# Splitting a turned table row group by two ScalarE copies and a GpSimd subtraction, in a two-block transformer kernel on one Trainium2 core

## The reference

```
def peer(xn, wq, subkeys, u, v):
    q = (xb @ wq).reshape(t, PEER_HEADS, 2, PEER_DQ // 2)
    s = jnp.einsum('thpd,hpkd->thpk', q, subkeys)
    ...                                   # top 16 of each half, top 16 of their sums -> e, g
    ue = jnp.take(u, e, axis=0)
    ve = jnp.take(v, e, axis=0)
    act = gelu(jnp.einsum('thkd,td->thk', ue, xb))
    return jnp.einsum('thk,thkd->td', g * act, ve)
```

## Time and profile before

| what | value |
|---|---|
| median of 3 runs (lowest, highest) | 2293.68 us (2287.43, 2296.37) |
| profiled execution | 2292.42 us, its span 2290.2 us |
| granted TensorE clock, mean | 0.960 |
| busy: PE, DVE, ACT, POOL | 2112.6, 1449.3, 767.0, 1075.8 us |
| DMA over the span | 514.89 MB, mean 225 GB/s |

### The profile page before, as it was taken

How to read it: one execution, slowest core, us unless ns; L and a number is a source line. 1 busy time by engine, 2 the same in 40 slices (tenths; PEclk the granted TensorE clock), 3 DMA queues, 4 the chain that set the end, 5 groups by cost and what they waited for, 6 DMA issues and landing times.

```text
span 2290.2 us, 29215 instructions
## 1 busy us (share of the span) xinstructions
PE 2112.6 (92%) x11218; PEld 1159.8 (51%) x11218; DVE 1449.3 (63%) x2649; ACT 767.0 (33%) x1089; POOL 1075.8 (47%) x610
## 2 busy tenths in 40 slices
PE   8999999999989999999799777998989989989998
PEld 4555544444444564555466534444444444444554
DVE  3669465464433743858989667776666666666554
ACT  3233333323332443211167623333333323333331
POOL 1001355566452346724022166665556656656661
PEclk9999999999999999999899988999999999999999
DMA  6030359898953218989379888887777777777752
GB/s 226 0 111 22 126 169 254 246 259 238 265 166 111 74 41 231 291 228 328 119 278 399 318 337 291 293 291 275 275 272 280 273 271 276 278 271 263 272 192 83
DMA packets 277573, 514.89 MB, mean 225 GB/s; under 512 B 131122, under 2 KB 188726, under 8 KB 266436
## 3 DMA queue, kind: packets, MB, share of 16 engines
q1 hardware_dynamic: 232516, 367.90, 49.0%
q0 software_dynamic: 36864, 134.23, 16.9%
q10 hardware_dynamic: 8064, 11.01, 1.4%
HBM read 416.09 MB, written 67.65 MB: 211 GB/s over the span
## 4 chain that ended last, share of the span: by engine, by line
PE 32%; DVE 11%; DMA 11%; POOL 4%; issue 3%; ACT 1%; SPq 1%; PEld 0%; POOLq 0%; DVEq 0%; ACTq 0%
PE ps L2127 11%; PE ps L2079 10%; DMA arena<-in_peer_u,small 5%; DMA arena<-in_peer_v,small 4%; PE ps L1750 4%; PE ps L2115 3%; PE ps L2069 2%; DVE arena L2783 2%; DVE x_sb L2787 2%; POOL split L943 2%; POOL arena L932 1%; DVE arena L2828 1%; DVE arena L2825 1%; DVE arena L2831 1%; PE ps L2054 1%
## 5 line engine op out<-in xcount | busy, mean ns | idle before, releaser
L2127 PE MATMUL ps<-split,arena 128*128 128x512 bf16 x1656 | 371.7, 380 | 21.9 <-DVE arena L2917 21.9
L943 POOL TENSOR_TENSOR split<-ring,split 128x1024 bf16<-128x1024 f32 x128 | 312.7, 2448 | 165.5 <-ACT split L1355 164.6
L2079 PE MATMUL ps<-arena 128*128 128x384 bf16 x1728 | 316.3, 343 | 0.7 <-ACT consts L1324 0.7
L1750 PE MATMUL ps<-arena,split 128*128 128x512 bf16 x1344 | 299.8, 381 | 3.0 <-DVE arena L2571 2.0
L816 POOL TENSOR_TENSOR split<-ring,split 128x4096 bf16<-128x4096 f32 x26 | 207.2, 7968 | 197.0 <-ACT split L1141 194.6
L932 POOL DMA_INDIRECT arena<-in_peer_u,small x128 | 158.0, 1234 | 259.1 <-DVE arena L2783 240.9
L2127 PEld LDWEIGHTS ps<-split,arena 128*128 128x128 bf16 x1656 | 162.2, 98 | 203.4 <-issue 22.1
L2787 DVE SCALAR_TENSOR_TENSOR x_sb<-arena,small,x_sb 128x1024 f32<-128x1024 f32 x128 | 208.2, 1627 | 61.8 <-DMA arena<-in_peer_v,small 59.8
L2783 DVE SCALAR_TENSOR_TENSOR arena<-arena,bcast 128x1024 f32<-128x1024 f32 x128 | 198.1, 1559 | 74.4 <-DMA arena<-in_peer_u,small 74.3
L2079 PEld LDWEIGHTS ps<-arena 128*128 128x128 bf16 x1728 | 178.0, 103 | 124.0 <-issue 25.7
L1750 PE MATMUL ps<-split,arena 128*128 128x512 bf16 x1056 | 231.6, 381 | 0.0
(11 more groups left out here) (335 smaller groups left out, 3000.3 us busy)
## 6 DMA issues: line engine op xcount, KB each, us to landing
ring<-in_peer_v SPq DMA_DIRECT2D x32, 2048.0 KB
ring<-in_peer_u SPq DMA_DIRECT2D x18, 2048.0 KB
ring<-in_w_ff SPq DMA_DIRECT2D x16, 2048.0 KB
arena<-in_peer_u SPq DMA_DIRECT2D x56, 512.0 KB, 4.8
turned_table<-u_split SPq DMA_DIRECT2D x56, 512.0 KB, 5.5
ring<-turned_table SPq DMA_DIRECT2D x14, 2048.0 KB
gate_matrix<-split SPq DMA_DIRECT2D x12, 2048.0 KB, 11.5
arena<-gate_matrix SPq DMA_DIRECT2D x32, 768.0 KB, 7.2
```

Of the source, the lines that this page charges most:

```text
L943: pool.tensor_tensor(split[:, s % 2, 1, at], ring[:, s % 2, at], split[:, s % 2, 0, at], ALU.subtract).then_inc(v_lo, 1)
L1750: mm = pe.matmul(dst, a(k), b(k), start=n == 0, stop=n == len(terms) - 1)
L2079: mm = pe.matmul(up_bank, a, b, start=n == 0, stop=n == len(terms) - 1)
L2127: mm = pe.matmul(down_bank(t, c), a, w, start=s == 0 and j == 0 and n == 0, stop=s == EX_GROUPS - 1 and j == 3 and n == 2)
```

## The change

A fill (from the ninth on, `FIRST = 8`) now leaves the PSUM bank by two copies of ScalarE: the bf16 high half as before, and the fp32 values as they are, into one of four buffers in SBUF (`turned_raw`). The next fill waits only for the second copy (semaphore `u_raw`). The low half is made by GpSimd from the buffer and the high half, and VectorE has no part in it. An up tile still waits for the low halves (`u_lo`). A raw copy waits until GpSimd has emptied the buffer used four fills earlier.

The orders of ScalarE, VectorE and GpSimd are written anew: `stored_high` and `live_high` stand later among ScalarE's fills; VectorE's `stored_times` move from the end of a pair to the beginning of the next. The first pair runs its four up tiles and four fills before the first down step. Three gathers stand earlier, before the first `v_low`. ScalarE's exponential for the gates stands after tile 22 instead of 17.

```diff
+        turned_raw = [part(base, at, 4, P) for base, at in ((u_room, 0), (u_room, 512), (consts, 2 * P), (consts, 2 * P + 512))]
...
+        FIRST = 8
...
-            gathers(0, 25)
+            def u_low(f):
+
+                if f >= 8 * LIVE:
+                    return
+                g, j, half = fill_place(f)
+                pool.wait_ge(u_raw, f - FIRST + 1)
+                pool.tensor_tensor(turned_u[:, 1, j, 4 * half:4 * half + 4, :], turned_raw[f % 4],
+                                   turned_u[:, 0, j, 4 * half:4 * half + 4, :], ALU.subtract).then_inc(u_lo, 1)
+
+            gathers(0, 28)
             for j in range(4):
                 v_low(0, j)
-            gathers(25, 28)
...
                 act.activation(turned_u[:, 0, j, 4 * half:4 * half + 4, :], turn_to, ACT.Copy).then_inc(u_hi, 1)
+                if f >= FIRST:
+                    if f >= FIRST + 4:
+                        act.wait_ge(u_lo, f - 3)
+                    act.activation(turned_raw[f % 4], turn_to, ACT.Copy).then_inc(u_raw, 1)
...
-                if m == 17:
+                if m == 22:
...
-                if f:
+                if f > FIRST:
+                    pe.wait_ge(u_raw, f - FIRST)
+                elif f:
                     pe.wait_ge(u_lo, f)
```

More of the change, by code:

```diff
@@ L953, in _ @@
                 for m in range(8):
-                    more = 2 if m < 7 or i < 3 else 0
+                    more = (4 if m == 0 else 2 if m < 7 else 0) if i == 0 else 2 if m < 7 or i < 3 else 0
                     gathers(n, n + more)
                     n += more
+                    for f in (((0, 1, 2, 3), (4,), (5,), (6,), (), (7,), (), ()) if i == 0 else ((0, 1), (2,), (3, 4), (5,), (6,), (7,), (), ()))[m]:
+                        u_low(8 * i + 8 + f)
                     v_low(2 * i + 1 + m // 4, m % 4)
@@ L961, in _ @@
                     n += 2
+                    for f in ((-1, 0), (1, 2), (3, 4), (5, 6))[j]:
+                        if f >= 0 or s > 2 * EARLY + 1:
+                            u_low(8 * (s - EARLY) + f)
                     v_low(s, j)
+            u_low(8 * LIVE - 1)
             gathers(n, 2 * PICKS)
@@ L1396, in _ @@
                 act.wait_ge(pre_stored[b], 32 * PRE)
-            for q in range(2):
-                act.wait_ge(gate_stored[q], 16 * (TD // TB // 2))
-            for j in range(4):
-                v_high(0, j)
-            for i in range(EARLY):
+            for b in range(3):
+                act.wait_ge(gelu_stored[b], 16 * ((4 * EARLY - b + 2) // 3))
+            live_gelu(EARLY, 0)
+            u_high(8)
+            act.wait_ge(gate_stored[0], 16 * (TD // TB // 2))
+            v_high(0, 0)
+            v_high(0, 1)
+            live_gelu(EARLY, 1)
+            u_high(9)
+            v_high(0, 2)
+            v_high(0, 3)
+            live_gelu(EARLY, 2)
+            u_high(10)
+            stored_high(0, 0)
+            stored_high(0, 1)
+            live_gelu(EARLY, 3)
+            u_high(11)
+            stored_high(0, 2)
+            stored_high(0, 3)
+            live_high(EARLY, 0)
+            live_high(EARLY, 1)
+            u_high(12)
+            live_high(EARLY, 2)
+            act.wait_ge(gate_stored[1], 16 * (TD // TB // 2))
+            v_high(1, 0)
+            v_high(1, 1)
+            u_high(13)
+            live_high(EARLY, 3)
+            v_high(1, 2)
+            u_high(14)
+            v_high(1, 3)
+            v_high(2, 0)
+            u_high(15)
+            v_high(2, 1)
+            for i in range(1, EARLY):
                 g, s, f = EARLY + i, 2 * i, 8 * i + 8
@@ L1433, in _ @@
                 u_high(f + 6)
+                live_high(g, 3)
                 v_high(s + 2, 0)
@@ L2144, in down @@
                 mm.then_inc(downs, 1)
-            for i in range(EARLY):
+            for j in range(4):
+                live_tile(EARLY, j)
+                turn_fill(FIRST + j)
+            pe.wait_ge(gate_out, TD // HB + 2)
+            for j in range(4):
+                down(0, j)
+                turn_fill(FIRST + 4 + j)
+            for i in range(1, EARLY):
                 g, s, f = EARLY + i, 2 * i, 8 * i + 8
@@ L2149, in _ @@
                 turn_fill(f)
[L2150 to L2154 removed]
+                down(s - 1, 0)
                 turn_fill(f + 1)
                 live_tile(g, 1)
[L2157 removed]
+                down(s - 1, 1)
                 turn_fill(f + 2)
@@ L2937, in _ @@
                 u_low(f)
+            rows_taken_to(24, 27)
             for j in range(4):
                 stored_times(0, j)
-            n = 24
-            for i in range(EARLY):
+            live_times(EARLY, 0)
+            stored_low(0, 0)
+            live_times(EARLY, 1)
+            stored_low(0, 1)
+            rows_taken_to(27, 28)
+            live_times(EARLY, 2)
+            stored_low(0, 2)
+            live_times(EARLY, 3)
+            stored_low(0, 3)
+            rows_taken_to(28, 29)
+            live_low(EARLY, 0)
+            rows_taken_to(29, 30)
+            live_low(EARLY, 1)
+            rows_taken_to(30, 31)
+            live_low(EARLY, 2)
+            rows_taken_to(31, 32)
+            live_low(EARLY, 3)
+            rows_taken_to(32, 35)
+            rows_taken_to(35, 40)
+            n = 40
+            for i in range(1, EARLY):
                 g, f = EARLY + i, 8 * i + 8
```

130 lines of the change are left out of this document (49 added, 81 removed).

## The result

| what | before | after |
|---|---|---|
| median, same chip (lowest, highest), 4 runs each | 2293.64 us (2287.43, 2296.37) | 2271.2 us (2268.38, 2274.14) |
| ratio to before, 95% interval | | 0.9906 [0.9882, 0.993] |
| profiled execution, span | 2292.42, 2290.2 us | 2268.38, 2266.6 us |
| granted TensorE clock, mean | 0.960 | 0.967 |
| busy: PE, DVE, ACT, POOL | 2112.6, 1449.3, 767.0, 1075.8 us | 2098.4, 1523.2, 825.0, 1249.4 us |

The account below looks back on a forecast made before the run. GpSimd was to set the pace after the change: pair 55.0 us against 58.0. Pairs 39 us, opening 12, last groups -3: 48 us off 2292.4 us gives 2244 us, range 2184 to 2300 us.

Parts of the forecast that it names:

- the wait for late rows, 6.2 us: GpSimd's wait per pair behind the two loads, 4.69 + 1.52 us, claimed to stay after the change.
- GpSimd's sum: GpSimd's time per pair after the change: 35.7 + 11.0 + 2.1 + 6.2 = 55.0 us, claimed to set the pace.
- used up: GpSimd's other waits, for V's copies and rows outside the collision, claimed to be slack from slower TensorE that disappears.
- VectorE's 39.4 us: VectorE's time per pair after the change, 40.1 - 5.5 + 8 x 0.6 us, claimed not to be a bound.
- The price of the subtraction: GpSimd's new low-half subtraction per fill: 1.05 + 0.33 = 1.38 us, 11.0 us a pair.
- Rival 2: Late rows hold VectorE's products and ScalarE's copies ahead of fills; pair stays 58.0 us, 2283 or 2295 us; chance 0.20.
- Each now stands several rows later: Argument against rival 2: products and their ScalarE copies come later in the new orders; no size given.
- Rival 1: TensorE becomes the bound in the pairs: pair 50.4 us, 2184 us; chance 0.22, with pairs under 53 us.
- Rival 3: GpSimd and VectorE exclude each other at the shared SBUF ports, so their work adds up in a pair; chance 0.13.
- The opening: First pair: 13.8 us of up tiles and fills moved into TensorE's 20.05 us wait; gain 12 us, bounds 0 and 13.8.
- The exponential: Moved behind tile 22: TensorE's 9.67 us wait becomes a longer wait for VectorE's picks; gain 0, bounds 0 and -3.
- The last groups: Last four groups: GpSimd 9.2 us a step against TensorE's 8.6 us; between 0 and 7 us slower, taken as 3.

Follow-up runs that it names:

- the memset runs: Changed kernel with GpSimd's subtraction for a fill replaced by three memsets of the same tile, 2266.19 us, or by two, 2209.45 us.
- rows_narrow: Changed kernel with VectorE's operations on gathered rows cut to 128 of 1024 columns, whole rows still gathered: 2182.6 us, ratio 0.9534.
- low_tiny: Changed kernel with GpSimd's subtraction for a fill cut to 8 of 128 columns, all waits and orders kept: 2186.73 us, ratio 0.9546.
- orders_only: Changed kernel's orders and opening with the old fill (low half by VectorE from PSUM, one ScalarE copy): 2305.94 us, ratio 1.0058.
- pieces_new_fill: Changed kernel with V and U loads cut into spaced 512 KB pieces, U pieces beside V pieces: 2220.01 us, ratio 0.9688.
- pieces_old_fill: Kernel before the change with V and U loads cut into spaced 512 KB pieces, U pieces beside V pieces: 2201.71 us, ratio 0.9604.

## Why the prediction was right in part and wrong in size

- **The failed step is the term "the wait for late rows, 6.2 us" in GpSimd's sum.** Measured, GpSimd waits 54.6 / 5 = 10.9 us a pair for VectorE to take rows. The other terms held: busy 45.4 us (46.7 predicted), gaps 1.6 (2.1). So 57.9 in place of 55.0 us: -1.3 - 0.5 + 4.7 = +2.9 us, and 13 x 2.9 = 38 of the 39 us that were to come from the pairs. The term was two waits of one stall, and the rest of GpSimd's waiting for rows was called slack and "used up". The trace of the kernel before had the whole of it. Its waits in five pairs, 1794.1 to 2084.2 us:

```profile
POOL arena L932 <- DVE x_sb L2787: 69.2, 35, 4.7
POOL split L943 <- ACT split L1355: 38.5, 20, 2.7
```

That is 13.8 us a pair for VectorE and 7.7 us for ScalarE. The second was slack and went whole; of the first only 2.9 us went. These 10.6 us made room for the 9.7 us of new work, and the pair stayed. The wait for VectorE closes a loop: the gathers wait for VectorE to take rows, VectorE waits for rows and is held by GpSimd.
- **Beside it, VectorE's 39.4 us.** It is 45.2 us. The time held at the ports was priced at 8 x 0.6 = 4.8 us; with 5.5 us of work gone and 5.1 us more busy time, it is 10.6 us. The operations that are held have changed too: `live_low` goes from 548 ns to 1750 ns, the stored products from 552 to 1580 ns, while `stored_low` falls from 1514 to 639 ns (1380 to 2200 us).
- **The price of the subtraction was right**: 1.38 us predicted, 1.34 to 1.36 measured, 1.16 to 1.17 us where VectorE left it alone. With a step of that length that doesn't touch VectorE the memset runs give 54.3 us, near my 55.0. The queue was summed rightly and the engines' hold on each other was not in it.
- **Rival 2 named what came**: ScalarE's copies of products, ahead of the fills' copies, wait for a VectorE that is late by a row; pair 58.0, for which the prediction had a chance of 0.20. It is also the sign of being wrong that the prediction named: a pair at 58 us with ScalarE waiting for VectorE ahead of a fill. "Each now stands several rows later" was no protection against 7.9 us. Its number came true by the loop: rows_narrow and low_tiny, each of which opens one side of the loop, both give 50 to 51 us.
- **Rival 1** needed the loop open; TensorE-bound pairs of 50.2 us appear there, close to its 50.4, at 2183 to 2187 us against its 2184. **Rival 3** was too dark: held time is there but costs 3.6 us a pair by the interpolation above, not 61 - 55. The Trainium skill, "SBUF — State Buffer", section "SBUF: two separate sides", calls the pair of ports that the two engines share an exclusive lock, held for a whole instruction; the 5.88 us for a 1.27 us operation agree with it. Rival 3's sum of both engines' work gave 61 us, and the measured pair is under that.
- **The opening**: 12 us predicted. The first pair gained 19.6, more than the 13.8 us of work moved: the first down step starts at 1321.05 us without a wait, and in place of the 20.05 us an up tile waits 7.43 for a GELU. The second lost 12.4, with the two waits below where the kernel before had one of 13.20 us:

```profile
1305.12 6.19 PE L2130 MATMUL ps<-arena 128*128 128x384 bf16 x24 [7.43 <-ACT u_split L1383]
1373.00 6.38 PE L2130 MATMUL ps<-arena 128*128 128x384 bf16 x24 [17.62 <-ACT u_split L1383]
1385.83 1.11 PE L2120 MATMUL ps<-consts,ring 128*128 128x128 f32 x4 [6.45 <-ACT consts L1366]
```

Net 7 us over two pairs. "Later rows may give it all back" stood as a bound; 12.4 of 19.6 us went back.

- **The exponential**: 0 predicted, and the 9.67 us came back whole at the next wait, 14.47 us where 3.31 us stood:

```profile
1130.78 0.90 PE L2152 MATMUL ps<-consts,arena 128*128 128x128 f32 x3 [14.47 <-DVE arena L2882]
```

- **The last groups**: 3 us slower predicted, 4.0 us faster measured, all in the first and, as orders_only shows, by the orders. GpSimd fits into TensorE's time, 61.63 of 65 us, and TensorE stays full, for the earlier trace rows:

```profile
2160.00:2225.00 65.00, 65.00 (x377) 37.69 (x376) 55.14 (x35) 28.34 (x51) 61.63 (x40) 1.00 0.52 169
```

My 1.24 us wait per step was one row taken for all.
- **Where the 22 us came from** is not where they were forecast. The steady pair gave about 1 of its 39 us; the gain lies in the opening, in pair 3, in the first of the last four groups and ahead of the final stage.

Left open: of the 24 us, 6.8 lie ahead of the final stage, 4.7 of them in unchanged code, and no run parts chance from cause there. The 3.6 us for the hold on VectorE are interpolated. The new fill in the old orders wasn't tried, so fill and orders are parted only by orders_only. Nor was the new opening with the old fill and pieces: the opening took 115.2 us for two pairs in pieces_new_fill and 131.5 us in pieces_old_fill.

## What to carry to other kernels

A wait that goes into a sum is read over a whole period, not in one stall, and it is a constant only if nothing in the change feeds back on it: where two engines wait for each other through a ring of buffers, sum each engine's busy time after the change, and if two of them come near the period, let both grow. Before moving work between engines at a stall, follow the stall to its start: here it was two large loads issued together ahead of gathered rows, and cutting and spacing those loads gave 4.0% with the fill left alone. When transfers are spaced, check the last piece against its first reader in the order of the engine that reads it.

## What the runs showed of the hardware that was not expected

- A memset of 128x512 bf16 on GpSimd took 0.53 us and left VectorE's 1024-column row operations at 1548 to 1577 ns; beside the fills' subtractions on GpSimd they took 1852 to 2101 ns. `v_low` ran in both.
- A VectorE operation on 128 of 1024 columns took 0.34 us alone and 1308 ns on average in this kernel: its length hardly counted beside the hold.
- A VectorE row operation of 1.27 us was held for 5.88 us over three GpSimd operations in a row (2.27 us for two and 2.12 us), though it started at 1837.49 us and the first of them at 1837.93 us.
- A gather of 512 KB took 16.49 us when two 2 MB loads were issued 1.9 us apart around it. With the loads in 512 KB pieces in the kernel before, VectorE's wait for rows fell from 50.3 to 12.9 us in 380 us, at 315 GB/s in place of 272.
